# Four pairs of joins one step later in the last merge, and one step of the state-space branch behind the fourth head's scores

## The reference

```python
h = rms_norm(x, g_norm[l]); z = h @ w_in[l]
q, k, v, fl, gf, u, gs, qm, gm, gl = split_cols(z)
y_fox = forgetting_attention(q, k, v, log_f) * silu(gf)      # 12 heads of 64
y_s5 = gelu(s5_ssm(u, ...)); y_s5 = y_s5 * sigmoid(y_s5 @ w_glu[l] + b_glu[l]) * silu(gs)
y_mem = memory_attention(qm, mk, mv) * silu(gm)
gates = sigmoid(gl + b_merge[l]).reshape(Bn, L, 3, D_MODEL)
merged = (gates[:, :, 0] * (y_fox @ w_proj_fox[l])
          + gates[:, :, 1] * (y_s5 @ w_proj_s5[l])
          + gates[:, :, 2] * (y_mem @ w_proj_mem[l]))
return rms_norm(x + merged @ w_out[l], g_final)
```

## Time and profile before

| | |
|---|---|
| median of 3 runs | 1979.88 us (1979.8 to 1979.91) |
| the profiled execution's own time | 1982.35 us |
| its span | 1981.0 us |
| busy: PE, DVE, ACT, POOL | 1933.5, 1196.1, 922.6, 943.7 us |
| mean granted clock of PE | 0.994 |

### The profile page before, as it was taken

The page is one execution under the profiler, slowest core; times in us unless marked ns, Lnnn a source line. Parts: engine busy times, 40 slices in busy tenths (PEclk is TensorE's granted clock), DMA queues, the critical chain, the costliest instruction groups (busy, mean ns, idle before and its releaser), DMA issues.

```text
span 1981.0 us, 28983 instructions
## 1 busy us (share of the span) xinstructions
PE 1933.5 (98%) x11395; PEld 1599.6 (81%) x11395; DVE 1196.1 (60%) x1924; ACT 922.6 (47%) x1747; POOL 943.7 (48%) x702
## 2 busy tenths in 40 slices
PE   5999999999999999999999999999999999999998
PEld 4868787878788877888788888888788777889986
DVE  5577879695466655674544440355765576876654
ACT  3555656564455544223444442344555454534442
POOL 1323323233543326564444545444474561788883
PEclk9999999999999999999999999999999999999999
DMA  8255353633322117664323334335222323233233
GB/s 308 65 171 181 112 184 118 184 123 126 96 61 65 47 32 286 235 234 149 107 87 105 92 95 141 98 118 182 64 72 73 89 57 112 85 99 95 90 121 137
DMA packets 92327, 242.48 MB, mean 122 GB/s; under 512 B 28192, under 2 KB 31392, under 8 KB 90784
## 3 DMA queue, kind: packets, MB, share of 16 engines
q1 hardware_dynamic: 88784, 231.98, 37.0%
q10 hardware_dynamic: 3408, 8.65, 1.1%
HBM read 223.14 MB, written 14.29 MB: 120 GB/s over the span
## 4 chain that ended last, share of the span: by engine, by line
PE 89%; POOL 3%; DVE 3%; ACT 2%; DMA 1%; SPq 1%; issue 1%; ACTq 0%; DVEq 0%
PE ps L972 21%; PE ps L973 20%; PE ps L981 20%; PE ps L1337 3%; PE ps L1412 2%; PE ps L1399 2%; PE ps L1474 1%; PE ps L1006 1%; PE ps L1005 1%; PE ps L1387 1%; PE ps L1314 1%; PE ps L1016 1%; PE ps L1071 1%; PE ps L1078 1%; PE ps L1072 1%; DMA modwb<-in_w_mod 1%
## 5 line engine op out<-in xcount | busy, mean ns | idle before, releaser
L3012 POOL TENSOR_TENSOR wlo<-raww,whi 128x512 fp32r<-128x512 f32 x217 | 303.4, 1398 | 681.5 <-ACT whi L1541 680.9
L1541 ACT CAST whi<-raww 128x1024 fp32r<-128x1024 f32 (+2 forms) x299 | 295.4, 995 | 201.6 <-PE ps L981 134.8
L3013 POOL TENSOR_TENSOR wlo<-raww,whi 128x512 fp32r<-128x512 f32 x217 | 310.0, 1429 | 0.0
L972 PE MATMUL ps<-hT_h,whi 128*128 128x512 f32 (+1 forms) x688 | 252.7, 377 | 1.2 <-ACT whi L1541 0.6
L973 PE MATMUL ps<-hT_l,whi 128*128 128x512 f32 (+1 forms) x688 | 245.6, 366 | 0.0
L981 PE MATMUL ps<-hT_h,wlo 128*128 128x512 f32 (+1 forms) x688 | 152.0, 363 | 0.0
L972 PEld LDWEIGHTS ps<-hT_h,whi 128*128 128x128 f32 x688 | 130.4, 190 | 25.9 <-issue 3.4
L973 PEld LDWEIGHTS ps<-hT_l,whi 128*128 128x128 f32 x688 | 130.5, 190 | 22.3 <-issue 1.9
L981 PEld LDWEIGHTS ps<-hT_h,wlo 128*128 128x128 f32 x688 | 119.3, 189 | 20.3
L972 PE MATMUL ps<-h_h,whi 128*128 128x512 f32 x336 | 130.7, 389 | 0.0
L973 PE MATMUL ps<-h_l,whi 128*128 128x512 f32 x336 | 130.7, 389 | 0.0
(11 more groups left out here) (637 smaller groups left out, 4870.4 us busy)
## 6 DMA issues: line engine op xcount, KB each, us to landing
ec<-csd SPq DMA_DIRECT2D x32, 1024.0 KB, 8.3
raww<-in_w_up SPq DMA_DIRECT2D x44, 512.0 KB, 3.6
modr<-in_w_mod SPq DMA_DIRECT2D x32, 512.0 KB, 5.6
raww<-in_w_xbc SPq DMA_DIRECT2D x24, 512.0 KB, 3.9
raww<-in_w_gl SPq DMA_DIRECT2D x24, 512.0 KB, 4.0
raww<-in_w_z SPq DMA_DIRECT2D x16, 512.0 KB, 3.8
raww<-in_w_g SPq DMA_DIRECT2D x16, 512.0 KB, 3.6
raww<-in_w_os SPq DMA_DIRECT2D x16, 512.0 KB, 4.0
```

The lines of the kernel that those rows point to most:

```text
L972: e.matmul(o, whi[:, i, c], hi(k)[:, t0:t1], start=(k == 0), stop=False)
L1541: e.copy(o, x.rearrange("p (k c) -> p k c", c=64) if p == plan.first["dt", 0] else x).then_inc(*w_high.mark(("high", p)))
L3012: e.tensor_tensor(o[:, 0:512], x[:, 0:512], h[:, 0:512].bitcast(F32), ALU.subtract).then_inc(*p_wlow.mark(("first half", p)))
L3013: e.tensor_tensor(o[:, 512:1024], x[:, 512:1024], h[:, 512:1024].bitcast(F32), ALU.subtract).then_inc(*p_wlow.mark(("split", p), ("raw fre ...
```

## The change

The first piece takes `("s5pow", 30)` and `("s5tab", 0)` out of the list and puts them back directly ahead of `("s5q", 0)`, behind the four score steps of head 3. The second moves each of joins 0 to 5 behind one more step `seven`. The third puts join 7 ahead of `("o2", 1)`.

```diff
@@ order()
     for step, other in AHEAD_OF:
         o.remove(step)
         o.insert(o.index(other), step)
+    for step in (("s5pow", 30), ("s5tab", 0)):
+        o.remove(step)
+        o.insert(o.index(("s5q", 0)), step)
     return o
@@ steps()
-    o += [("o2", 0), ("join", 6), ("o2", 1), ("join", 7), ("o2", 2), ("o2", 3), ("xback",)] + [("o2", k) for k in range(4, 8)]
+    o += [("o2", 0), ("join", 6), ("join", 7), ("o2", 1), ("o2", 2), ("o2", 3), ("xback",)] + [("o2", k) for k in range(4, 8)]
@@ gates_of_branches()
-                    o += [("seven", q, j, i)] + [("join", 2 * j + i - 3)] * (q == 0 and i in (1, 2))
+                    o += [("seven", q, j, i)] + [("join", 2 * j + i - 4)] * (q == 0 and i in (2, 3))
```

## The result

The changed kernel takes 1983.67 us (median of 21 runs) beside 1980.11 us for the kernel before on the same chip: the ratio is 1.0016, with a 95% interval of 1.0011 to 1.0022. By the interval it is 2.2 to 4.4 us slower: a loss clear of the noise, and a little more than the +2.0 us of the forecast. The medians differ by 3.56 us, which is 0.18% and so inside the 0.2% that I had called no change (the interval's upper end is just outside it); the range up to 1984.3 holds the 1983.67. The profiled execution has a span of 1984.8 us.

A forecast was written before the change was run, and what follows sets the result against it. The kernel was taken as bound by PE (busy 1933.5 of 1981.0 us). Terms -0.6 + 3.0 - 0.4 = +2.0 us gave a median of 1981.9 us, called no change; 8-in-10 range 1976.3 to 1984.3.

The forecast's parts named there:

- The case I had called likeliest: The forecast itself: joins cost 0.4 to 1.3 us each, other places give 0.6 to 2: 1979.0 to 1983.6; chance 0.62.
- First place: Scores of head 3: maxima start 4.5 us earlier, PE starts scores at 1431.9, then waits for `BA`: -0.6 us.
- Gain: 0.13 us by the earlier release, and 0.45 for the four transposes, 0.6 in all: At head 3's scores, PE's gain before it waits for `BA`'s second half: 0.6 us if the low clock comes back.
- Of the 2.3 I count 1.6, because the maxima of head 4 come behind the subtraction L2053 and a copy on DVE, and these move forward by 1.6 us only: At head 3's scores, if the low clock doesn't come back: gain up to 2.3 us, of which 1.6 counted.
- costs 4.0 x 0.43 = 1.7 us more: Behind head 3's scores in the kernel before: mean granted clock 0.57 from 1435 to 1439 costs 1.7 us.
- The forecast's signs: Expected in the profile: no bracket at L1474, `BA` wait 1.2 to 1.5 us, clock dip behind it, two POOL pauses about 1.3.
- Second place: Joins in `seven, 0, j`, three times: the 0.40 us wait goes, but the next gate block's splits come late: +3.0 us.
- the walk: Timing of joins 0 and 1 through DVE, POOL and ACT: PE 0.9 to 1.0 us later at each place's third split.
- Rival 2: At the joins, the waits vanish and nothing replaces them: 1974.9 to 1977.7, at best 1976.5; chance 0.24.
- Third place: Last product, join 7 following join 6: PE's matmul L1159 begins at 1942.5 and not 1942.87: -0.4 us.
- The wait for `o2h`: In the last product, a new PE wait of 0.4 us: ACT rounds the first block until 1937.5, PE wants it at 1937.11.
- Rival 3: At the joins, POOL's lateness exceeds what one stage absorbs: +2.3 to +2.7 us a place, 1986.4 whole; chance 0.14.

The follow-up runs named there:

- joins at one and three: Kernel before with only the second join of each pair moved, by two steps (join 0 behind seven 1 as before, join 1 behind seven 3): 1980.99 us (1 run).
- kernels with `BA` early: Six POOL operations on `BA` put ahead of gf 0, against the kernel before: alone 1979.61 us; powers moved too 1977.33; all gaining pieces 1974.28, or 1978.09 with s5q first.

## Why the prediction was right or wrong

**No change within 0.2%, and +2.0 against +3.6.** Right in the outcome, with some luck. The case I had called likeliest has the mechanism of the second and third place right and that of the first wrong, and the first place alone is 2.3 us off (-0.6 against +1.7), more than the whole +2.0. The measured 1983.67 lies just above that case's own band of 1979.0 to 1983.6 (its terms give 1983.2 as the upper end), and only the wider range to 1984.3 holds it.

**First place: wrong.** The record has -0.6. In the three traces with this order the start of `tm` is 0.17 us later and not earlier, and in the two in which the clock fell on the `tm` products the piece costs 1.7 and 1.8 in all. (The timed +1.06, with -0.8 to +2.8, doesn't exclude -0.6 by itself.) The step that failed is "Gain: 0.13 us by the earlier release, and 0.45 for the four transposes, 0.6 in all": I followed PE up to the transposes and put what comes behind them at nothing. Two waits stand there, 0.48 for the DVE copy, which I had myself left in its old place, and 1.82 for ACT's copy to `qk`; they take back all that was gained. "Of the 2.3 I count 1.6, because the maxima of head 4 come behind the subtraction L2053 and a copy on DVE, and these move forward by 1.6 us only" fails for the same reason. They don't move forward at all: L2053 stood at 1438.41 and stands at 1438.25, in a frame that is 0.32 earlier. It waits for ACT's rounding, which stands on ACT behind the scaling of head 3's last block, and that waits for the fourth reciprocal, which the moved powers keep at its old time. I had followed DVE's queue and POOL's, and said rightly that DVE's later work stays where it is; I had not followed ACT's queue from there. The run with the scaling first shows it: with the fourth reciprocal and the copy ahead of the powers the start of `tm` is 2.68 us earlier.

Nor was the low clock priced rightly: "costs 4.0 x 0.43 = 1.7 us more" is what the products took longer, not what it cost, since PE would have waited 1.35 us for `qk` otherwise. After the change it does cost: 1.64 us behind T in the trace with the powers alone (1.81 less the 0.17 at T), as it falls on products with nothing to wait for, and 1.5 in the changed kernel. Whether it falls differs between executions: of three traces with the moved powers two have it. Why is not shown.

The forecast's signs were right in part: no bracket at the scores, 1.54 for `BA` (1.2 to 1.5 said), and a dip of the clock behind it, but on `tm` and not on the scores.

**Second place: right, +3.0 said, +2.8 to +2.9 shown.** The 0.96 a stage, two pauses of 1.3, and join 1's end came within 0.1 us of the walk; PE waits 0.9 where the signs said 1 or more. What the walk took for granted and the runs add: POOL's part by itself, moved like that, is worth -0.63 a stage. Rival 2 was right on the wait and wrong on the joins; in a kernel that moves only POOL's part, it is what happens. (Its "at best 1976.5" doesn't fit its own range of 1974.9 to 1977.7; nothing hangs on it.)

**Third place: right, -0.4 said, -0.46 to -0.51 shown.** The wait for `o2h` was 0.22 and not 0.4, and that for `o2l` nothing and not 0.4. The later transfers on SP cost nothing that shows.

**Rival 3** (one more POOL instruction ahead of the split, 1986.4) didn't come. What lifts the time above the forecast is the first place, which no rival had.

## What to carry to other kernels

When a step is moved ahead of what PE waits for, follow the queue of every engine that it passes, the third one too: nothing is gained before the last of the queues ends, and here that was ACT behind a reciprocal on DVE. Small DVE operations that look long in a trace should be asked what POOL does beside them before they are moved; taking POOL's work away from beside them gave more at X1 (2.45 us) than moving them behind the scaling (0.91). When a list orders all engines at once, split a step by engine: the place of the joins that was good on POOL (-0.63 us a stage) was bad on DVE and ACT (+0.97 with it).

## What was not expected of the hardware

Operations of DVE on 24 columns took 0.18 us with POOL idle (three in 0.62) and mostly 0.9 to 1.3 when they met one of its instructions (three in 2.62 and 2.69); two maxima that read `ps` took 0.62 either way. A join operation on 512 columns took 0.7 us alone and up to 2.2 beside a 768 block, always ending 0.55 behind it. A fall of the clock to 1.2 GHz can be free: 19.30 us with it and 19.31 without, when another engine decides. It fell in some executions of one and the same program and not in others, at this place: of the traces whose program is that of the kernel before up to there, the one before and the one with joins at one and three have it, the three with only joins, join 7 or POOL's rest changed do not. What decides it is left open. And Z itself, with nothing changed ahead of it but in the kernels with `BA` early, lay between 1416.53 and 1420.24 us from the start, so that spans of single executions can't be compared to a microsecond, and distances inside them can.
